# Moving the down-projection weights of a streamed mixture-of-experts block from SyncE's DMA queue to ScalarE's

## The chip, the cores and the metric

One core of a Trainium2 chip runs the whole kernel. The metric is the device time of one execution in microseconds (us). All data is float32: the weights are streamed from HBM (the chip's main memory) into the core's on-chip memory once, and the expert weights are more than three quarters of all bytes.

## The reference, cut to what matters

One decoder layer for 256 tokens of width 2048: an input projection, two groups of attention heads, an output projection, cross attention into 256 memory tokens, then a mixture of experts, and a final norm. The change touches the mixture of experts only:

```
# 32 experts, D_MODEL = 2048, D_EXPERT = 512; top-1 group of 8 experts, then top-2 in it
a = jnp.einsum('td,edf->tef', t, w_gate)            # w_gate (32, 2048, 512)
u = jnp.einsum('td,edf->tef', t, w_up)              # w_up   (32, 2048, 512)
act = jax.nn.silu(a) * u * combine[:, :, None]
y = jnp.einsum('tef,efd->td', act, w_down)          # w_down (32, 512, 2048)
...
return rms_norm(x + y, norm_final)
```

Every expert's three matrices are 4.19 MB each (2048 x 512 x 4 bytes), 12.58 MB per expert.

## The kernel before, in words

The kernel is written out by hand, one instruction stream for each engine, joined by semaphores. Each engine runs its own stream strictly in order. The streams of SyncE (SP), TensorE (PE), ScalarE (ACT), VectorE (DVE) and GpSimd (POOL) are the functions under `@block.sync`, `@block.tensor`, and so on.

**The experts' loop.** Experts 0 to 31 are processed one after the other, with 32 token slots each (all tokens fit in one pass over the experts with these inputs). On PE, `expert(n, ...)` does in this order: `combine` of the previous expert's first half of the tokens, `gate_up(0)` (the first half of the 2048 input rows against gate and up weights), `combine` of the second half, `gate_up(1)`, `gather` and `gather_turn` for the next expert's tokens, three transposes, `project_down`, which multiplies with the down weights in four quarters (j = 0 to 3). The last expert has its own function, `last_expert`, with four extra matmuls (`residual`) instead of the gather. ScalarE does the SiLU (sg), copies the gathered slots (x_slots), copies bank 6 (turned), and at the end copies the expert output from bank 7 to `y_sb`, which PE's next `combine` waits for. VectorE multiplies and adds the result to `x_res`.

**The buffers.** Gate and up weights have two buffers, `gu[0]` and `gu[1]`, of one whole expert each (8.39 MB). Down weights have one buffer for one expert (4.19 MB), in two halves `down0` and `down1`. The semaphores `gu_used0` and `gu_used1` count how often the first and second half of a gate/up buffer was read, `down_used0` and `down_used1` the same for the halves of the down buffer. `gu_loaded..` and `down_loaded0` to `down_loaded3` say that data have landed.

**The order of the loads.** Before the change all expert weights are issued by SP. `load_gate_up(e, side, used)` issues 4 DMAs of 2.1 MB: for each half b it waits for `gu_used{b}` to reach `used`, then issues gate and up. `load_down(e, used)` issues 4 DMAs of 1.05 MB, one for each quarter, and waits for `down_used0` and `down_used1`. In the steady loop (L411 to L415) SP issues expert e's gate and up once expert e-2 has read its own, and then expert e's down once expert e-1 has read its own; since SP runs in order, the gate and up of e+1 are issued only behind the down of e. On the queue the order is gate/up e, down e, gate/up e+1, down e+1. Nothing but the queue order decides what the DMA engines move next. The last load on that queue is the final gain `g_fin` (L428).

A row of gate or up of one DMA is 8 x 512 x 4 = 16384 bytes for each of 128 partitions, a row of down is 2048 x 4 = 8192 bytes.

Of the kernel before, what the change touches and what calls it, by code (L numbers as in the profile page):

```python
# [25 lines left out]
P = 128  # L26
# [7 lines left out]
EXPERTS = GROUPS * PER_GROUP  # L34
FE = 512
SLOTS = 32
NJ = P // SLOTS
MAX_PASSES = SEQ // SLOTS
AHEAD = 3
# [31 lines left out]
def chunk_cols(c):  # L71
    return KV_RANK + ROPE if c == KV_LAT else UN
# [40 lines left out]
def layer(nc, x, mem, positions, norm_mix, w_in, norm_q_lat, w_q_b, norm_kv_lat, w_kv_b,  # L113
# [6 lines left out]
    def S(name):  # L120
        if name not in sems:
            sems[name] = ctx.enter_context(nc.semaphore(name))
        return sems[name]

    with ctx:
# [4 lines left out]
        def place(name, shape, dt=F32, offset=None):  # L130
            size = 4
            for s in shape[1:]:
                size *= s
            if offset is None:
                offset = at[0]
                at[0] += size + (-size) % 64
            assert offset + size <= limit, (name, offset + size, limit)
            return nc.alloc_sbuf_tensor_at(name, shape, dt, offset=offset)
# [64 lines left out]
        down0 = place("down0", [P, 2, D], offset=e_at + 4 * 16 * 1024)  # L203
        down1 = place("down1", [P, 2, D], offset=a_lo_at)
# [106 lines left out]
        n = 0  # L311
# [30 lines left out]
        def _(sp):  # L342
# [13 lines left out]
            for u, (c, i) in enumerate(UNITS):  # L356
# [8 lines left out]
                dst = w_raw[:, u % RING, :, 0:chunk_cols(c)]  # L365
# [8 lines left out]
            def load_gate_up(e, side, used=None, halves=(0, 1)):  # L374

                wg = w_gate[0, e].rearrange("(p k) f -> p (k f)", k=KD)
                wu = w_up[0, e].rearrange("(p k) f -> p (k f)", k=KD)
                half = KD // 2 * FE
                for b in halves:
                    if used is not None:  # L380
                        sp.wait_ge(S(f"gu_used{b}"), used)
                    for m, w in enumerate((wg, wu)):
                        sp.dma_start(gu[side][:, b, m].rearrange("p k f -> p (k f)"),  # L383
                                     w[:, b * half:(b + 1) * half]).then_inc(
                                         S(f"gu_loaded{side}{b}"), 16)

            def load_down(e, used=None):
                wd = w_down[0, e].rearrange("(j p) d -> p j d", p=P)
                for b, dst in enumerate((down0, down1)):
                    if used is not None:  # L390
                        sp.wait_ge(S(f"down_used{b}"), used)
                    for jj in range(2):
                        sp.dma_start(dst[:, jj, :], wd[:, 2 * b + jj, :]).then_inc(  # L393
                            S(f"down_loaded{2 * b + jj}"), 16)

            sp.wait_ge(S("w_used"), START[MEM_O])
            sp.wait_ge(S("mem_scores"), MEM_HEADS)

            load_gate_up(0, 0)
            load_down(0)  # L400
            sp.wait_ge(S("w_used"), len(UNITS))
            sp.wait_ge(S("w_split"), len(UNITS))
            load_gate_up(1, 1)
            for e in range(2, AHEAD):
                load_gate_up(e, e % 2, e - 1)
                load_down(e - 1, e - 1)
            load_gate_up(AHEAD, AHEAD % 2, AHEAD - 1, halves=(0,))
            load_down(AHEAD - 1, AHEAD - 1)
            load_gate_up(AHEAD, AHEAD % 2, AHEAD - 1, halves=(1,))
            load_down(AHEAD, AHEAD)  # L410
            with sp.Fori(0, (EXPERTS - AHEAD - 1) // 2) as i:  # L411
                for m in range(2):
                    e = 2 * i + AHEAD + 1 + m
                    load_gate_up(e, (AHEAD + 1 + m) % 2, 2 * i + AHEAD + m)
                    load_down(e, 2 * i + AHEAD + 1 + m)  # L415
            sp.wait_ge(S("routed"), 1)
            total = sp.value_load(n_iter[0:1, 0:1], min_val=EXPERTS, max_val=MAX_PASSES * EXPERTS)
            with sp.If(total > EXPERTS):

                with sp.Fori(EXPERTS - 1, total - 1, EXPERTS) as before_:  # L420
                    with sp.Fori(0, EXPERTS // 2) as i:
                        for side in range(2):
                            load_gate_up(2 * i + side, side, before_ + 2 * i + side)
                            load_down(2 * i + side, before_ + 2 * i + 1 + side)
            total_1 = sp.value_load(n_iter[0:1, 1:2], min_val=EXPERTS - 1,
                                    max_val=MAX_PASSES * EXPERTS - 1)
            sp.wait_ge(S("gu_used1"), total_1)
# [477 lines left out]
        def _(sc):  # L905
# [268 lines left out]
            def slots_copy(n, first=False):  # L1174
                sc.wait_ge(S("gathered"), n + 1)
                if not first:
                    sc.wait_ge(S("slots_turned"), n)
                sc.activation(x_slots[:, :], ps[4][:, :], ACT.Copy).then_inc(S("slots_copied"), 1)  # L1178

            def expert(n, m=None):  # L1180

                sc.wait_ge(S("gu_used1"), n + 1)
                if m is not None:
                    sc.wait_ge(S("act_ready"), n)
                sc.activation(sg[:, :], ps[5][:, 0:P], ACT.Silu).then_inc(S("silu"), 1)  # L1185
                slots_copy(n + 1)
                sc.wait_ge(S("bank6_turned"), n + 1)
                if m is not None:
                    sc.wait_ge(S("combined"), TT * m + TT)
                    sc.wait_ge(S("down_used1"), n)  # L1190
                sc.activation(turned_6[:, :, :], ps[6][:, 0:(TT + 1) * P].rearrange(  # L1191
                    "p (t a) -> p t a", t=TT + 1), ACT.Copy).then_inc(S("bank6_copied"), 1)
                sc.wait_ge(S("down_used1"), n + 1)
                sc.activation(y_sb[:, :], ps[7][:, :], ACT.Copy).then_inc(S("y_copied"), 1)  # L1194

            slots_copy(0, first=True)
            sc.wait_ge(S("routed"), 1)
# [2 lines left out]
            before_last = sc.value_load(n_iter[0:1, 3:4], min_val=EXPERTS - 2,  # L1200
                                        max_val=MAX_PASSES * EXPERTS - 2)
            expert(0)
            with sc.Fori(0, before_last) as m:
                expert(m + 1, m)
# [550 lines left out]
        def _(gp):  # L1755
# [32 lines left out]
            def norms(cols, width, made, count):  # L1788

                gp.wait_ge(S(made), count)  # L1790
                for col in cols:
                    r = rstd[:, col:col + TT]
                    link(gp.tensor_scalar(r, sums[:, col:col + TT], 1.0 / width, EPS, ALU.mult, ALU.add))
                    ins = gp.tensor_tensor(r, r, minus_half[:, :], ALU.pow)
                ins.then_inc(S("rstd"), 1)
# [38 lines left out]
                    allow_small_or_imprecise_dtypes=True).then_inc(S("router_consts"), 1)  # L1834
            norms([SS_X2], D, "sums_made", 3)
            gp.wait_ge(S("rstd"), 7)
            def apply_gain(g):

                gp.wait_ge(S("last_added"), g + 1)
                cols = slice(g * UN, (g + 1) * UN)  # L1840
                gp.tensor_tensor(x_gain[:, g, :], x_res[:, 1, cols], g_fin[:, cols],
                                 ALU.mult).then_inc(S("gain_applied"), 1)

            gp.wait_ge(S("final_gain_loaded"), 16)
            for t in range(TT):
                apply_gain(t)
                gp.wait_ge(S("final_summed"), t + 1)
                link(gp.tensor_scalar(rstd[:, t:t + 1], sums[:, t:t + 1], 1.0 / D, EPS, ALU.mult,
                                      ALU.add))
                gp.tensor_tensor(rstd[:, t:t + 1], rstd[:, t:t + 1], minus_half[:, 0:1],  # L1850
                                 ALU.pow).then_inc(S("final_rstd"), 1)
            apply_gain(2)


# [24 lines left out]
```

## Time and profile before

| | |
|---|---|
| runs | 1423.21, 1419.56, 1421.71 us; median 1421.71 |
| the profiled execution | 1421.97 us, its span 1420.2 us |
| busy in the span | PE 75%, PE weight loads 45%, DVE 38%, ACT 24%, POOL 2% |
| moved | 481.69 MB in 87203 packets, 479.04 MB of it read from HBM |
| on SP's queue (q1) | 478.75 MB, 84.2% of the 16 DMA engines' time |
| on ACT's queue (q10) | 2.11 MB, 0.4% |
| experts' loop | from about 496 us to 1405 us |

The span is the time between the first and the last recorded instruction. The page's 40 slices are 35.5 us each. PE is the matrix engine and PEld its weight loads; an engine's name with q behind it (SPq, ACTq) is that engine issuing a DMA, L383 is line 383 of the kernel. In a row of waits, "A <- B" is time in which A's engine stood still until B was done.

### The profile page before, as it was taken

The numbers are of one execution on the slowest core, as the hardware profiler recorded it, in microseconds if no ns is written. First come the engines' busy times: TensorE is split into PE (matmuls) and PEld (weight loads), VectorE is DVE, ScalarE is ACT, GpSimd is POOL, SyncE is SP. The second block draws the span as 40 slices with busy tenths as digits, with TensorE's granted clock in tenths as the row PEclk, the third lists the DMA queues.
The fourth block names the chain that finished last, engine by engine and source line by source line (L and its number), as shares of the span: only waits on it lengthen the run. The fifth ranks groups of instructions, "written<-read, shape, count | busy, mean of one in ns | idle before, by whom it ended". The sixth has DMA issues, their size and how long they took to land.

```text
span 1420.2 us, 21509 instructions
## 1 busy us (share of the span) xinstructions
PE 1071.1 (75%) x8704; PEld 637.2 (45%) x8704; DVE 534.0 (38%) x1108; ACT 336.7 (24%) x608; POOL 33.1 (2%) x95
## 2 busy tenths in 40 slices
PE   7999999999998888665666666666566665666665
PEld 6888887888886633222222222222222222232222
DVE  5544576666654533222222222222222222222222
ACT  5554456665454400000000000000000000000002
POOL 1000001110001000000000000000000000000001
PEclk9999999999999888888888888888888888888888
DMA  7766653225558889999999999999999999999996
GB/s 234 256 201 184 178 164 119 95 70 193 188 181 317 334 358 424 427 427 427 426 424 429 425 427 425 425 426 427 427 425 425 427 427 426 426 425 428 426 426 265
DMA packets 87203, 481.69 MB, mean 339 GB/s; under 512 B 11318, under 2 KB 21692, under 8 KB 54012
## 3 DMA queue, kind: packets, MB, share of 16 engines
q1 hardware_dynamic: 86668, 478.75, 84.2%
q10 hardware_dynamic: 304, 2.11, 0.4%
q0 software_dynamic: 192, 0.31, 0.2%
q8 instruction: 25, 0.41, 0.1%
q14 instruction: 14, 0.11, 0.0%
HBM read 479.04 MB, written 2.10 MB: 339 GB/s over the span
## 4 chain that ended last, share of the span: by engine, by line
DMA 43%; PE 37%; SPq 6%; ACT 5%; DVE 3%; issue 2%; POOL 0%; ACTq 0%; POOLq 0%; DVEq 0%
DMA gu<-in_w_up 41%; PE ps L489 7%; PE ps L491 7%; PE ps L490 7%; PE ps L794 5%; SPq L383 5%; PE ps L847 4%; PE ps L775 2%; DMA down<-in_w_down 2%; DVE w_lo L1252 1%; SPq L393 1%; PE ps L784 1%; ACT x_slots L1178 1%; PE ps L456 1%; PE ps L512 1%
## 5 line engine op out<-in xcount | busy, mean ns | idle before, releaser
L794 PE MATMUL ps<-gu,xe 128*32 128x256 f32 x4096 | 319.9, 481 | 240.2 <-DMA gu<-in_w_up 239.2
L794 PEld LDWEIGHTS ps<-gu,xe 128*32 128x32 f32 x4096 | 153.7, 137 | 428.2 <-DMA gu<-in_w_up 286.4
L1646 DVE TENSOR_TENSOR x_res<-ps,x_res 128x512 f32<-128x512 f32 x248 | 154.0, 683 | 411.3 <-PE ps L804 411.3
L1252 DVE TENSOR_TENSOR w_lo<-w_raw,w_hi 128x1024 fp32r<-128x1024 f32 (+1 forms) x138 | 164.1, 1200 | 134.3 <-ACT w_hi L918 131.3
L489 PE MATMUL ps<-w_hi,a_hi 128*128 128x512 f32 (+1 forms) x512 | 202.0, 395 | 5.7 <-DVE w_lo L1252 3.8
L490 PE MATMUL ps<-w_lo,a_hi 128*128 128x512 f32 (+1 forms) x512 | 198.1, 387 | 0.0
L491 PE MATMUL ps<-w_hi,a_lo 128*128 128x512 f32 (+1 forms) x480 | 185.2, 386 | 0.0
L918 ACT ACTIVATE w_hi<-w_raw 128x1024 fp32r<-128x1024 f32 (+1 forms) x138 | 142.1, 1039 | 140.9 <-PE ps L491 132.4
L1185 ACT ACTIVATE sg<-ps 128x128 f32<-128x128 f32 x31 | 8.6, 278 | 613.2 <-PE ps L794 613.2
L847 PE MATMUL ps<-down,turned 128*32 128x512 f32 x1024 | 120.3, 609 | 26.7 <-ACT turned L1191 23.6
L489 PEld LDWEIGHTS ps<-w_hi,a_hi 128*128 128x128 f32 x512 | 97.0, 189 | 26.9 <-issue 5.5
L490 PEld LDWEIGHTS ps<-w_lo,a_hi 128*128 128x128 f32 x512 | 97.0, 189 | 18.0
L491 PEld LDWEIGHTS ps<-w_hi,a_lo 128*128 128x128 f32 x480 | 90.4, 188 | 18.2
L804 PE MATMUL ps<-y_sb,turned 32*128 32x512 f32 x496 | 71.7, 647 | 23.5 <-ACT y_sb L1194 23.5
L847 PEld LDWEIGHTS ps<-down,turned 128*32 128x32 f32 x1024 | 30.8, 110 | 94.4 <-issue 81.1
L1676 DVE TENSOR_TENSOR act<-sg,ps 128x128 f32<-128x128 f32 x31 | 8.9, 288 | 159.1 <-ACT sg L1185 159.1
L775 PE MATMUL ps<-h_nat,hot 128*32 128x512 f32 x512 | 62.5, 607 | 1.3 <-DVE hot L1628 1.3
L1637 DVE TENSOR_TENSOR xe<-ps,g_ffn 128x128 f32<-128x128 f32 x128 | 28.3, 283 | 78.1 <-PE ps L784 78.1
L804 PEld LDWEIGHTS ps<-y_sb,turned 32*128 32x128 f32 x496 | 20.0, 185 | 64.8 <-issue 38.8
L1194 ACT ACTIVATE y_sb<-ps 128x512 f32<-128x512 f32 x31 | 18.5, 597 | 124.8 <-PE ps L847 124.8
L784 PE MATMUL ps<-ident,x_slots 128*128 128x128 f32 x128 | 21.4, 291 | 23.0 <-ACT x_slots L1178 23.0
L784 PEld LDWEIGHTS ps<-ident,x_slots 128*128 128x128 f32 x128 | 13.7, 143 | 52.9 <-ACT x_slots L1178 52.9
(276 smaller groups left out, 771.4 us busy)
## 6 DMA issues: line engine op xcount, KB each, us to landing
gu<-in_w_gate SPq DMA_DIRECT2D x64, 2048.0 KB, 31.6
gu<-in_w_up SPq DMA_DIRECT2D x64, 2048.0 KB, 36.0
down<-in_w_down SPq DMA_DIRECT2D x128, 1024.0 KB, 23.6
w_raw<-in_w_in SPq DMA_DIRECT2D x56, 512.0 KB, 4.4
w_raw<-in_w_out SPq DMA_DIRECT2D x32, 512.0 KB, 3.8
w_raw<-in_w_mem_kv SPq DMA_DIRECT2D x16, 512.0 KB, 3.9
w_raw<-in_w_mem_q SPq DMA_DIRECT2D x8, 512.0 KB, 3.3
w_raw<-in_w_mem_o SPq DMA_DIRECT2D x8, 512.0 KB, 3.6
```

The lines of the kernel that those rows point to most:

```text
L383: sp.dma_start(gu[side][:, b, m].rearrange("p k f -> p (k f)"), w[:, b * half:(b + 1) * half]).then_inc(S(f"gu_loaded{side}{b}"), 16)
L489: pe.matmul(acc[t][:, 0:n], xh, wh, start=(k == 0), stop=False)
L490: pe.matmul(acc[t][:, 0:n], xh, wl, start=False, stop=False)
L491: mm = pe.matmul(acc[t][:, 0:n], xl, wh, start=False, stop=(k == kn - 1))
L775: mm = pe.matmul(ps[4][g * SLOTS:(g + 1) * SLOTS, :], hot[:, t, :], h_nat[:, t, 4 * g:4 * g + 4, :].rearrange("p k d -> p (k d)"), start=( ...
L784: mm = pe.transpose(ps[4][:, j * P:(j + 1) * P], x_slots[:, j * P:(j + 1) * P], ident[:, :])
L794: mm = pe.matmul(ps[5][j * SLOTS:(j + 1) * SLOTS, 0:2 * P].rearrange("s (m f) -> s m f", m=2), xe[:, k, :], gu[side][:, b, :, kk, j * P:(j ...
L804: return pe.matmul(ps[g][:, :], turned_6[rows, t, :], y_sb[rows, :], start=True, stop=True)
L847: mm = pe.matmul(ps[7][g * SLOTS:(g + 1) * SLOTS, :], act_t[:, j * SLOTS:(j + 1) * SLOTS], w[:, jj, g * UN:(g + 1) * UN], start=(j == 0), ...
L918: sc.activation(w_hi[:, u % RING, :, 0:n], w_raw[:, u % RING, :, 0:n], ACT.Copy).then_inc(S("w_rounded"), 1)
L1252: ve.tensor_tensor(w_lo[:, u % RING, :, 0:n], w_raw[:, u % RING, :, 0:n], w_hi[:, u % RING, :, 0:n], ALU.subtract).then_inc(S("w_split"), 1)
L1646: ins = ve.tensor_tensor(xs, ps[g][:, :], xs, ALU.add)
```

## The change

`load_down` goes from SP's stream. A new `load_first_down` issues expert 0's down weights on SP, where they were. All other experts' down weights are issued by ScalarE at the end of its `expert(n)`: behind the copy of `y_sb`, with a wait for `down_used0` in front (the wait for `down_used1` stands before the copy already). SP's loop has only `load_gate_up` left, with the same waits. The buffers, the semaphores and the computation stay as they were.

```diff
-            def load_down(e, used=None):
-                wd = w_down[0, e].rearrange("(j p) d -> p j d", p=P)
-                for b, dst in enumerate((down0, down1)):
-                    if used is not None:
-                        sp.wait_ge(S(f"down_used{b}"), used)
-                    for jj in range(2):
-                        sp.dma_start(dst[:, jj, :], wd[:, 2 * b + jj, :]).then_inc(
-                            S(f"down_loaded{2 * b + jj}"), 16)
+            def load_first_down():
+                wd = w_down[0, 0].rearrange("(j p) d -> p j d", p=P)
+                for j in range(NJ):
+                    sp.dma_start((down0, down1)[j // 2][:, j % 2, :], wd[:, j, :]).then_inc(
+                        S(f"down_loaded{j}"), 16)
...
             load_gate_up(0, 0)
-            load_down(0)
+            load_first_down()
             sp.wait_ge(S("w_used"), len(UNITS))
             sp.wait_ge(S("w_split"), len(UNITS))
             load_gate_up(1, 1)
             for e in range(2, AHEAD):
                 load_gate_up(e, e % 2, e - 1)
-                load_down(e - 1, e - 1)
-            load_gate_up(AHEAD, AHEAD % 2, AHEAD - 1, halves=(0,))
-            load_down(AHEAD - 1, AHEAD - 1)
-            load_gate_up(AHEAD, AHEAD % 2, AHEAD - 1, halves=(1,))
-            load_down(AHEAD, AHEAD)
+            load_gate_up(AHEAD, AHEAD % 2, AHEAD - 1)
             with sp.Fori(0, (EXPERTS - AHEAD - 1) // 2) as i:
                 for m in range(2):
                     e = 2 * i + AHEAD + 1 + m
                     load_gate_up(e, (AHEAD + 1 + m) % 2, 2 * i + AHEAD + m)
-                    load_down(e, 2 * i + AHEAD + 1 + m)
...
                 sc.wait_ge(S("down_used1"), n + 1)
                 sc.activation(y_sb[:, :], ps[7][:, :], ACT.Copy).then_inc(S("y_copied"), 1)
+                sc.wait_ge(S("down_used0"), n + 1)
+                wd = w_down[0, 1 if m is None else (m + 2) % EXPERTS].rearrange("(j p) d -> p j d", p=P)
+                for j in range(NJ):
+                    sc.dma_start((down0, down1)[j // 2][:, j % 2, :], wd[:, j, :]).then_inc(
+                        S(f"down_loaded{j}"), 16)
```

The order of the instructions in SP's steady loop before, one expert of the two that the loop holds (the line numbers are those of each kernel; an ISA row is a register or wait instruction; gu is the gate/up buffer, down the down buffer):

```order
L383 ISA [waits gu_used0]
L383 DMA gu_96<-in_w_gate 128x4096
L383 DMA gu_96<-in_w_up 128x4096
L383 ISA [waits gu_used1]
L383 DMA gu_96<-in_w_gate 128x4096
L383 DMA gu_96<-in_w_up 128x4096
L393 DMA down_98<-in_w_down 128x2048 [waits down_used0]
L393 ISA
L393 DMA down_98<-in_w_down 128x2048
L393 ISA [waits down_used1]
L393 DMA down_99<-in_w_down 128x2048
```

And the same loop now, two experts:

```order
L383 ISA [waits gu_used0]
L383 DMA gu_96<-in_w_gate 128x4096
L383 DMA gu_96<-in_w_up 128x4096
L383 ISA [waits gu_used1]
L383 DMA gu_96<-in_w_gate 128x4096
L383 DMA gu_96<-in_w_up 128x4096
L383 ISA [waits gu_used0]
L383 DMA gu_97<-in_w_gate 128x4096
L383 DMA gu_97<-in_w_up 128x4096
```

What moved: no down load and no wait for the down buffer stands between two experts' gate/up loads any more. ScalarE's loop over the experts, now:

```order
L1176 ACTIVATE sg<-ps 128x128 [waits act_ready]
L1166 REGISTER_ALU
L1169 ACTIVATE x_slots<-ps 128x512 [waits slots_turned,gathered]
L1180 ISA [waits bank6_turned]
L1182 ACTIVATE turned_130<-ps 128x384 [waits down_used1,combined]
L1185 ACTIVATE y_sb<-ps 128x512 [waits down_used1]
L1189 ISA [waits down_used0]
L1189 DMA down_98<-in_w_down 128x2048
L1189 ISA
L1189 DMA down_98<-in_w_down 128x2048
```

What moved: the four down loads (two shown) stand behind the copy of the expert output; before, the loop ended with that copy.

## Rows read from the trace of the kernel before

**Rows 1.** The page: DMA share and GB/s in 40 slices; DMA queues
```profile
DMA  7766653225558889999999999999999999999996
GB/s 234 256 201 184 178 164 119 95 70 193 188 181 317 334 358 424 427 427 427 426 424 429 425 427 425 425 426 427 427 425 425 427 427 426 426 425 428 426 426 265
```
**Rows 2.** The waits, 500 to 1400 us: us in total, times, longest
```profile
PEld ps L794 <- DMA gu<-in_w_up: 286.4, 57, 7.2
PE ps L794 <- DMA gu<-in_w_up: 239.2, 57, 6.4
...
PEld ps L847 <- DMA down<-in_w_down: 12.5, 18, 2.3
```
**Rows 3.** DMA queues in 1376 to 1391 us: packets, MB, share of 16 engines
```profile
q1 hardware_dynamic: 474, 6.38, 100.1%
```
**Rows 4.** Windows, one expert each: engines busy, PEclk, DMA share, GB/s
```profile
900.00:929.50 29.50, 19.66 (x219) 8.02 (x215) 8.56 (x24) 1.96 (x4) 0.00 (x0) 0.88 1.01 427
1332.00:1361.50 29.50, 20.13 (x199) 8.38 (x199) 7.12 (x20) 1.96 (x4) 0.00 (x0) 0.83 1.01 426
```
**Rows 5.** Windows at the loop's start: engines busy, PEclk, DMA share, GB/s
```profile
498.00:502.00 4.00, 4.00 (x52) 1.98 (x48) 0.52 (x2) 0.00 (x0) 0.00 (x0) 0.64 0.03 12
...
505.00:520.00 15.00, 12.97 (x155) 5.05 (x147) 5.56 (x17) 1.96 (x4) 0.00 (x0) 1.00 1.01 429
```
**Rows 6.** Timeline around the end of expert 30 and expert 31: start, us, engine
```profile
1362.13 3.66 PE L794 MATMUL ps<-gu,xe 128*32 128x256 f32 x64 [2.49 <-DMA gu<-in_w_up]
...
1370.01 3.64 PE L847 MATMUL ps<-down,turned 128*32 128x512 f32 x32 [0.79 <-ACT turned L1191]
...
1373.71 0.60 ACT L1194 ACTIVATE y_sb<-ps 128x512 f32<-128x512 f32 x1 [3.83 <-PE ps L847]
...
1374.36 1.14 PE L804 MATMUL ps<-y_sb,turned 32*128 32x512 f32 x8 [0.71 <-ACT y_sb L1194]
...
1391.67 5.35 PE L794 MATMUL ps<-gu,xe 128*32 128x256 f32 x64 [3.60 <-DMA gu<-in_w_up]
...
1400.91 3.64 PE L847 MATMUL ps<-down,turned 128*32 128x512 f32 x32
1404.62 0.60 ACT L1215 ACTIVATE y_sb<-ps 128x512 f32<-128x512 f32 x1 [5.55 <-PE ps L847]
```
**Rows 7.** SP's issues at the end of the experts' loop
```profile
1344.15 2.70 SPq L393 DMA_DIRECT2D down<-in_w_down  x4
1347.04 0.33 SPq L383 DMA_DIRECT2D gu<-in_w_gate  x1
1347.47 0.38 SPq L383 DMA_DIRECT2D gu<-in_w_up  x1
1348.04 3.63 SPq L383 DMA_DIRECT2D gu<-in_w_gate  x1
1351.76 4.19 SPq L383 DMA_DIRECT2D gu<-in_w_up  x1
1371.99 2.70 SPq L393 DMA_DIRECT2D down<-in_w_down  x4
```
**Rows 8.** ScalarE's only large DMA and its landing; SP's next issues
```profile
56.58 0.42 ACTq L1014 DMA_DIRECT2D mem_sb<-in_mem  x1
...
59.44 1.50 SPq L372 DMA_DIRECT2D w_raw<-in_w_in  x2
...
DMA to landing us min/median/max: 10.3/10.3/10.3
```
**Rows 9.** DMA queues in 57 to 59 us, 61 to 63 us and 63 to 65 us
```profile
q1 hardware_dynamic: 341, 0.67, 93.8%
...
q10 hardware_dynamic: 91, 0.75, 98.6%
...
q10 hardware_dynamic: 85, 0.70, 83.8%
q1 hardware_dynamic: 72, 0.15, 18.9%
```
**Rows 10.** Gate/up loads, all: us from issue to landing
```profile
DMA to landing us min/median/max: 7.2/35.5/40.0
```
**Rows 11.** Window 64 to 65 us, both queues at work
```profile
64.00:65.00 1.00, 1.00 (x7) 0.81 (x6) 1.00 (x1) 0.00 (x0) 0.00 (x0) 1.00 1.09 449
```

More of the change, by code:

```diff
@@ L423, in _ @@
                             load_gate_up(2 * i + side, side, before_ + 2 * i + side)
-                            load_down(2 * i + side, before_ + 2 * i + 1 + side)
             total_1 = sp.value_load(n_iter[0:1, 1:2], min_val=EXPERTS - 1,
```

## The prediction

> **What bounds the kernel now.** I began with the page's slices [rows 1]: from slice 17 (about 600 us) the DMA share reads 9 in every slice and the rate stands at 424 to 429 GB/s, while section 1 of the page gives no engine more than 75%. Then the waits [rows 2]: in the experts' loop PE and its weight loads stand still for gate/up data (the two rows count the same time twice, once for each), and for down data for 12.5 us in all. The windows of single experts confirm it: 29.5 us long, DMA share 1.01, 426 or 427 GB/s, PE busy for only some 20 us [rows 4]. One expert is 12.58 MB, and 12.58 MB / 0.427 MB per us = 29.5 us. So the loop is a queue of bytes that is never empty, and whoever asks for a time must ask three things: are the same bytes moved, is the queue ever empty, and how much work is left on PE when it has run out. The chain of waits cannot answer the last, the timeline at the end can [rows 6].
>
> **The end before.** Gate/up of expert 31 has landed at 1391.67, where PE starts on its second half [rows 6]. Behind it on the queue were only the down weights of 31, 4.19 MB, 9.8 us: the transfers end at about 1401.5. PE meanwhile needs 5.35 us of gate_up and some four us of small steps and residual matmuls, so that project_down starts at 1400.91 and takes its usual 3.64 us [rows 6]; the down load is hidden. y_sb is copied at 1405.22, and everything behind it (combine, norm, store) is the same before and after.
>
> **The change, part by part.**
> SP loses 124 down issues of 0.68 us (2.70 us for four [rows 7]) and its waits for the down buffer. SP stands waiting most of the time, so this is worth nothing by itself. What follows from it: gate/up of e+2 is no longer held until project_down of e has half finished; it is issued right behind gate_up of e, some 7 us sooner. No buffer is added, so gate/up can be ahead by two experts at most, as before, but it now stands in its queue before the down weights of e+1.
> ScalarE gains 4 issues for each of 31 experts. Its one large DMA took 0.42 us to issue [rows 8]; SP's pitch gives 0.68. That is 1.7 to 2.7 us per expert, behind the y_sb copy, so PE's combine isn't held up, and before ScalarE's next work (the SiLU behind both gate_up halves, 1.14 + 3.66 + 1.14 + 3.66 = 9.6 us later at the soonest). Even issues that stall as SP's did (up to 4.19 us [rows 7]) would come to under 17 us, and would be felt only in part. I take 0. The added wait for down_used0 is met when that for down_used1 is.
> The down weights of e+1 are now asked for when all of project_down(e) and the copy are done, not when its first half is: 1.8 + 0.7 us later. What counts is how the two queues share the engines.
>
> **How the queues share.** Only once does the trace show ScalarE's queue at work beside SP's: the 2.1 MB load of 56.58 us, landed after 10.3 us [rows 8]. In 61 to 63 us it has the engines alone; in 63 to 65 us both move, 85 packets of 8 KB (0.70 MB) beside 72 of 2 KB (0.15 MB) [rows 9]. That is packet for packet, not byte for byte. The packets of gate/up are 16 KB rows (in 1376 to 1391 us, 474 packets, of which 50 are tiny completions, carry 6.38 MB, 15 KB each [rows 3]), those of down 8 KB rows. Packet for packet, gate/up gets two thirds and down one third. The Trainium skill says the same of the switching ("DMA: Bandwidth & Descriptors", Queues, rings and completion order: each DMA engine takes turns between its rings at packet granularity); by bytes in equal parts the sum would be 9.8 us, the first rival below, instead of 14.7.
>
> At one third, 0.142 MB/us, the down weights need 29.5 us from the first byte. Between one expert's down landing and the next one's first byte lie the last quarter of project_down (0.91), the copy and its hand-over (0.71), and the start of a DMA (7.2 us is the shortest landing of 2.1 MB [rows 10], less 4.9 us for the bytes: 2.3, part of it at the landing end): 3.5 to 4 us. 29.5 + 3.8 is more than the 29.5 us of an expert's bytes, so down becomes what PE waits for, by some 11 us per expert, and gate/up runs ahead until its two buffers are full and its queue runs dry; then down has the engines alone and catches up. As long as gate/up has 1.6 MB (3.8 us) in its queue when a down load lands, no time is lost: 29.5 us per expert as before. At the start of the loop the transfers pause before 502 us, waiting for the first expert, and are busy from 505 us on [rows 5]; that stays. **Steady part: 0.**
>
> **The end after, which makes the sum.** Gate/up has run ahead, so what is left at the end is down alone, and down cannot run ahead: one buffer. When down of 29 lands, in the extreme case only down of 30 and 31 are unmoved, 19.6 us of transfers; all else has been moved without a pause, so this is at 1401.5 - 19.6 = 1381.9. From there PE goes: last quarter 0.91, copy and hand-over 0.71, then twice a whole expert at PE's own pace. One is 1.14 + 3.66 + 1.14 + 3.66 (combines and gate_up) + 4.22 (1365.79 to 1370.01) + 3.64 + 0.71 = 18.2 us, all from [rows 6]. Down of 30 and 31 take 9.8 + 2.3 us and their issues and just hide in it. 1381.9 + 1.6 + 36.4 = 1419.9 against 1405.2: **+14.7 us**. The near bound: gate/up of 31 and down of 30 land together at 1401.5 - 9.8 = 1391.7; 1.6 + 18.2 behind that is 1411.5, **+6.3**. The far one: both experts' gate_up at 5.35 instead of 3.66 us, as after PE's idle time in [rows 6]: 4 x 1.7 more, +21.5. I take +14.7, because a gate/up queue with two thirds of the rate runs dry first. On the profiled execution of 1421.97 that is 1436.7, on the median of 1421.71 it is **1436.4 us**.
>
> **Rivals.**
> 1. *Gate/up lands last.* If down gets half of the bytes or more (for it: in 61 to 63 us ScalarE's queue had 98.6% [rows 9] although SP had issued more from 59.44 on [rows 8]), down is in early and gate/up of 31 ends the transfers at 1401.5 instead of 1391.67. PE's 13.5 us behind it stay: +9.8, 1431.5. Or it ends at the near bound, +6.3, 1428. Chance 0.30.
> 2. *Starved down.* If gate/up gets more than two thirds, or the start of a DMA is longer than 2.3 us behind full engines (issued at 56.58 [rows 8], ScalarE's load had moved nothing before 59 [rows 9]), the gate/up queue is empty when down lands, and both stand still for 3.8 us. At one expert in three: 10 x 3.8 = 38, 1421.7 + 14.7 + 38 = 1474; at every expert 1550. It decides as soon as less than 1.6 MB is queued at the landing. Chance 0.10.
> 3. *More rate from two queues, faster.* One microsecond with both at work shows 449 GB/s [rows 11] against 427. Behind 502 us the loop has 30 x 8.39 + 31 x 4.19 = 382 MB, 894 us at 427; at 449 it is 44 us less, and with the tail 1421.7 - 44 + 14.7 = 1392. It decides from 1.6% on. Against it: the engines are at 1.01 busy with one queue already, and 63 to 65 us around that microsecond show 0.85 MB in 2 us. Chance 0.04.
> 4. *Nothing.* Same bytes, same engines: if gate/up doesn't run ahead, and the last down still comes last, the end is as before, 1421.7. The Trainium skill speaks for this (same page, Issuing engines are not separate DMA queues: DMAs of several engines interleave on the same 16, and a second one saves only issue time). The new queue order speaks against it: SP no longer holds gate/up of 31 until project_down(29). Chance 0.06.
>
> **How the numbers follow.** Forecast 0.50, rivals 0.30, 0.10, 0.04, 0.06. A measurement of this kernel can tell 0.3%, 4.3 us. The forecast and rivals 1 and 2 are slower by more: 0.90; rival 4 the same 0.06; rival 3 faster 0.04. The range takes in the near bound, 1428, and the far one, 1443, with two or three gaps of 3.8 us: 1427 to 1452; rivals 2, 3 and 4, 0.20, lie outside.
>
> **What would show it.** In the changed kernel's profile: ScalarE's queue at about 130 MB and SP's at about 349; the windows of single experts still 29.5 us and 427 GB/s; PE's wait for down grown from 12.5 us to some 300, that for gate/up nearly gone; single down loads landing 20 to 30 us after the issue; in the last 40 us a DMA share well under 1, with PE at 18 us for each of the two last experts. Gate/up waits as before and a last gate/up landing near 1401 would make it rival 1; windows under 427 GB/s in mid-loop, rival 2; over 430, rival 3.

## The result and the profile after

The changed kernel takes 1435.87 us (median of 5, 1430.77 to 1437.76) against 1421.84 us of the kernel before in the same series: 14.0 us more, ratio 1.0091 with a 95% interval of 1.0073 to 1.011. In a second series (e5 below) it was 1432.26 against 1423.4 us, ratio 1.007 (1.0048 to 1.0091). So the medians put the cost of the change at 14 us once and at 9 us once. The prediction was 1436.4 us.

The profiled execution took 1436.69 us, its span is 1435.0 us. The page, against [rows 1]: the DMA share, the rates, and the queues.

```profile
DMA  7766653225558799999999999999999999999994
GB/s 228 249 209 182 182 165 120 92 80 185 190 178 339 298 386 423 427 425 418 430 425 427 424 422 426 427 427 408 425 426 427 427 426 424 426 429 424 426 397 176
...
q1 hardware_dynamic: 68812, 348.72, 61.8%
q10 hardware_dynamic: 18160, 132.14, 22.3%
```

348.72 MB are left on SyncE's queue, 132.14 MB are on ScalarE's, and from slice 15 to slice 37 (counted from 0) the engines are almost as busy as before (two slices fall short, 418 and 408 GB/s). The last two slices are not: 397 and 176 GB/s, where [rows 1] has 426 and 265. The same in windows (columns as in [rows 4]): 740 us of the loop's middle of the kernel before, then of the changed one,

```profile
600.00:1340.00 740.00, 471.20 (x4975) 194.37 (x4975) 193.42 (x500) 49.13 (x101) 0.00 (x0) 0.85 1.01 426
```

```profile
600.00:1340.00 740.00, 479.13 (x4975) 177.66 (x4975) 193.50 (x500) 49.09 (x100) 0.00 (x0) 0.79 1.01 425
...
1390.00:1400.00 10.00, 5.66 (x24) 0.61 (x24) 0.00 (x0) 0.00 (x0) 0.00 (x0) 0.53 0.68 282
1400.00:1410.00 10.00, 9.28 (x120) 4.04 (x120) 4.21 (x7) 0.60 (x1) 0.00 (x0) 0.79 0.85 342
1410.00:1420.00 10.00, 9.33 (x79) 3.46 (x71) 1.05 (x3) 1.36 (x3) 0.00 (x0) 1.00 0.19 79
```

In the middle 425 against 426 GB/s: almost nothing lost. The bytes moved in 520 to 1380 us say how much, first before, then changed:

```profile
DMA packets 33800, 366.44 MB, mean 426 GB/s; under 512 B 3754, under 2 KB 3754, under 8 KB 3754
```

```profile
DMA packets 33464, 365.42 MB, mean 425 GB/s; under 512 B 3712, under 2 KB 3712, under 8 KB 3712
```

1.02 MB fewer is 2.4 us of the engines' time (0.64 MB and 1.5 us in e5, the changed kernel's second trace). At the end the engines run at 0.68, 0.85 and 0.19 while PE is busy; that is the larger part. The waits in the loop, against [rows 2]:

```profile
PEld ps L838 <- DMA down<-in_w_down: 314.5, 59, 7.2
PE ps L838 <- DMA down<-in_w_down: 244.0, 57, 6.3
```

No row for gate/up is left; PE waits for down instead, and for about as long in all (244.0 us against 239.2 in [rows 2]). Who is waited for has changed altogether, and the mean time of an expert has hardly changed. How the queues share (bytes and packets in 904 to 910, 912 to 918 and 918 to 926 us):

```profile
q1 hardware_dynamic: 164, 2.42, 94.9%
q10 hardware_dynamic: 15, 0.12, 4.8%
...
q10 hardware_dynamic: 334, 2.44, 97.7%
q1 hardware_dynamic: 12, 0.15, 5.8%
...
q1 hardware_dynamic: 160, 2.36, 69.3%
q10 hardware_dynamic: 146, 1.03, 31.0%
```

First gate/up nearly alone, while down pauses; then down nearly alone, because gate/up has filled its buffers; then both, 160 packets beside 146, which is 2.36 MB beside 1.03 MB. (The packet counts hold a few tiny completions.) The timeline at the end, against [rows 6]:

```profile
1371.23 1.06 PE L838 MATMUL ps<-down,turned 128*32 128x512 f32 x8 [0.61 <-DMA down<-in_w_down]
1372.36 0.60 ACT L1185 ACTIVATE y_sb<-ps 128x512 f32<-128x512 f32 x1 [4.65 <-PE ps L838]
1372.54 1.92 ACTq L1189 DMA_DIRECT2D down<-in_w_down  x4
...
1398.21 1.93 PE L838 MATMUL ps<-down,turned 128*32 128x512 f32 x8 [0.52 <-DMA down<-in_w_down]
1400.21 0.60 ACT L1185 ACTIVATE y_sb<-ps 128x512 f32<-128x512 f32 x1 [13.62 <-PE ps L838]
1400.38 2.04 ACTq L1189 DMA_DIRECT2D down<-in_w_down  x4
...
1402.88 4.26 PE L785 MATMUL ps<-gu,xe 128*32 128x256 f32 x64
...
1408.14 3.66 PE L785 MATMUL ps<-gu,xe 128*32 128x256 f32 x64
...
1415.69 3.64 PE L838 MATMUL ps<-down,turned 128*32 128x512 f32 x32
1419.40 0.60 ACT L1211 ACTIVATE y_sb<-ps 128x512 f32<-128x512 f32 x1 [5.55 <-PE ps L838]
```

Both gate_up halves of expert 31 start with no wait for data; down 31 is asked for only at 1400.38, and PE then needs a whole expert at its own pace. The last y_sb is copied at 1420.0 us, before at 1405.22: 14.8 us later. Of these, 2.1 us were there before the change could cost anything: expert 0's y_sb is copied at 515.85 us, where the trace of before has 513.77, and what PE does up to there is the same code on data loaded as before. That this is chance is seen over the runs: the same copy stands between 509.7 us (e3) and 516.4 us (e7) in the traces of all kernels here. So the traces are compared below from this copy on. From expert 0's copy to expert 31's it is 904.2 us against 891.5, **12.7 us more**. They split like this: up to expert 30's copy 885.0 against 860.5 us (24.4 more), and then 19.2 against 30.9 us for the last expert (11.7 given back).

### The profile page after: what moved, and what is told of

It reads as the page before. It is cut to its first block, busy times and chain, and to the rows that moved or that the text cites. A ratio compares the mean times of both kernels' runs of the same rounds, so it can differ in the third digit from the quotient of the medians.

```text
span 1435.0 us, 21555 instructions
## 1 busy us (share of the span) xinstructions
PE 1083.3 (75%) x8704; PEld 619.8 (43%) x8704; DVE 534.1 (37%) x1108; ACT 336.9 (23%) x608; POOL 33.1 (2%) x95
## 3 DMA queue, kind: packets, MB, share of 16 engines
q1 hardware_dynamic: 68812, 348.72, 61.8%
q10 hardware_dynamic: 18160, 132.14, 22.3%
## 4 chain that ended last, share of the span: by engine, by line
DMA 49%; PE 35%; ACT 4%; DVE 3%; ACTq 2%; issue 2%; POOL 0%; POOLq 0%; DVEq 0%
DMA down<-in_w_down 49%; PE ps L480 7%; PE ps L482 7%; PE ps L481 7%; PE ps L838 5%; PE ps L785 4%; ACTq L1189 2%; DVE w_lo L1248 1%; PE ps L795 1%; PE ps L766 1%; PE ps L447 1%; PE ps L503 1%; ACT w_hi L909 1%; ACT head_junk L1047 1%; ACT y_sb L1185 0%
## 5 line engine op out<-in xcount | busy, mean ns | idle before, releaser
L838 PE MATMUL ps<-down,turned 128*32 128x512 f32 x1024 | 166.8, 759 | 268.4 <-DMA down<-in_w_down 244.0
L785 PE MATMUL ps<-gu,xe 128*32 128x256 f32 x4096 | 265.1, 417 | 1.0 <-DVE xe L1633 1.0
L785 PEld LDWEIGHTS ps<-gu,xe 128*32 128x32 f32 x4096 | 134.3, 120 | 167.4 <-issue 98.8
L838 PEld LDWEIGHTS ps<-down,turned 128*32 128x32 f32 x1024 | 26.5, 119 | 368.8 <-DMA down<-in_w_down 314.5
L795 PE MATMUL ps<-y_sb,turned 32*128 32x512 f32 x496 | 94.1, 836 | 23.6 <-ACT y_sb L1185 23.6
L795 PEld LDWEIGHTS ps<-y_sb,turned 32*128 32x128 f32 x496 | 24.7, 231 | 83.0 <-issue 49.6
L1169 ACT ACTIVATE x_slots<-ps 128x512 f32<-128x512 f32 x32 | 19.1, 597 | 44.7 <-PE ps L766 44.7
## 6 DMA issues: line engine op xcount, KB each, us to landing
gu<-in_w_up SPq DMA_DIRECT2D x64, 2048.0 KB, 24.5
down<-in_w_down ACTq DMA_DIRECT2D x124, 1024.0 KB, 14.8
```

Of the source, the lines that this page charges most:

```text
L785: mm = pe.matmul(ps[5][j * SLOTS:(j + 1) * SLOTS, 0:2 * P].rearrange("s (m f) -> s m f", m=2), xe[:, k, :], gu[side][:, b, :, kk, j * P:(j ...
L795: return pe.matmul(ps[g][:, :], turned_6[rows, t, :], y_sb[rows, :], start=True, stop=True)
L838: mm = pe.matmul(ps[7][g * SLOTS:(g + 1) * SLOTS, :], act_t[:, j * SLOTS:(j + 1) * SLOTS], w[:, jj, g * UN:(g + 1) * UN], start=(j == 0), ...
```

## The experiments

**e1: one queue, gate/up ahead.** The kernel before, with each down load issued behind the gate/up load of the expert after it.

```diff
-                    load_down(e, 2 * i + AHEAD + 1 + m)
+                    load_down(e - 1, 2 * i + AHEAD + m)
...
+            load_down(EXPERTS - 1, EXPERTS - 1)
```

> All down loads are on SyncE's queue again, but behind the gate/up loads of the expert after, so that gate/up runs ahead and nothing is shared between two queues. Theory A (the time went to the end of the loop, because gate/up has run ahead and the last down load needs its buffer): the order gate/up 31, down 30, down 31 costs the near bound of the prediction, +6 us (4 to 9), and single experts still take 29.5 us at 427 GB/s. Theory B (the second queue itself costs, by sharing or by ScalarE's issues): as the kernel before, within 2 us.

Measured: 1430.89 us against 1421.9, ratio 1.0052 (1.0037 to 1.0068), which is 5 to 10 us. Its waits and its middle:

```profile
PE ps L844 <- DMA down<-in_w_down: 232.4, 120, 7.5
```

```profile
600.00:1340.00 740.00, 505.28 (x4999) 172.14 (x4991) 193.47 (x500) 49.05 (x100) 0.00 (x0) 0.78 1.01 426
```

There is no second queue here, and half and more of the loss is there, with 232 us of waits for down (244 in the changed kernel) and the same rate in the middle. Gate/up ahead of down is enough to lose at the end. Theory B falls as the whole cause; whether the second queue adds a few us of its own the times can't tell, since this interval overlaps that of the changed kernel's second series. The 9 us are over the near bound of 6.3, and the trace shows why. From expert 0's copy to expert 31's it is 900.1 us, 8.7 more than before. PE had been waiting for expert 30's down weights, and at the start of expert 31 its granted clock is 0.68 (1393.9 to 1400.6 us):

```profile
1393.88 2.09 PE L801 MATMUL ps<-y_sb,turned 32*128 32x512 f32 x8 [0.70 <-ACT y_sb L1191]
1395.90 4.79 PE L791 MATMUL ps<-gu,xe 128*32 128x256 f32 x64
```

At the full clock the two take 1.14 and 3.66 us [rows 6]. These 2.1 us on top of 6.3 make 8.4.

**e2: down rows of 4 KB.** The changed kernel, each down DMA cut in two by columns, on both queues; PE waits for 32 instead of 16 per quarter.

```diff
+                    for c in range(2):
+                        cs = slice(c * D // 2, (c + 1) * D // 2)
+                        sc.dma_start((down0, down1)[j // 2][:, j % 2, cs], wd[:, j, cs]).then_inc(
+                            S(f"down_loaded{j}"), 16)
```

> The changed kernel with each down load cut in two, with rows of 4 KB in place of 8 KB; the bytes are the same. If the two queues take turns packet by packet, down gets one fifth of the rate beside gate/up (4 KB to 16 KB) in place of one third, gate/up is out when down lands, and the engines stand still: 30 to 130 us slower than the changed kernel, with windows of single experts clearly under 427 GB/s. If they share by bytes, or by time in equal parts, the time is that of the changed kernel within 3 us.

Measured: 1514.12 us, ratio to the kernel before 1.0673 (1.0633 to 1.0713), some 80 us above the changed kernel. The queues in 1040 to 1044 us, and the middle window:

```profile
q1 hardware_dynamic: 100, 1.38, 81.1%
q10 hardware_dynamic: 103, 0.36, 22.1%
```

```profile
600.00:1340.00 740.00, 445.64 (x4589) 167.08 (x4593) 179.74 (x469) 45.61 (x93) 0.00 (x0) 0.77 0.95 391
```

100 packets beside 103, 1.38 MB beside 0.36: packet for packet again, and now down has a fifth. The rate falls to 391 GB/s: this is the starved down of the prediction's rival 2, made to happen by cutting the rows. The cut also doubles the number of down DMAs. The packet counts speak for the rows as the cause, and the doubled gate/up DMAs of e3 cost nothing like it, but no run has twice the DMAs with rows of the old size.

**e3: gate/up rows of 8 KB.** The changed kernel, each gate/up DMA cut in two, PE waiting for 64 instead of 32.

> The changed kernel with each gate/up load cut in two, with rows of 8 KB in place of 16 KB. Packet by packet, down then gets one half of the rate: it lands within 20 us, PE's waits move from down (244 us) back to gate/up, windows stay at 427 GB/s, and the end is rival 1 of the prediction, gate/up of 31 landing last: +8 to +18 us against the kernel before. By bytes or time: waits for down stay at some 240 us.

Measured: 1441.02 us (of five runs one at 1433.24, the profiled one, and four from 1440.57 to 1441.22), ratio 1.0135 (1.0118 to 1.0152): +19 us. Queues in 1040 to 1044 us, waits, and the middle:

```profile
q1 hardware_dynamic: 118, 0.85, 51.2%
q10 hardware_dynamic: 117, 0.83, 49.7%
```

```profile
PE ps L788 <- DMA gu<-in_w_up: 237.0, 29, 13.9
...
PE ps L841 <- DMA down<-in_w_down: 31.4, 12, 4.1
```

```profile
600.00:1340.00 740.00, 450.47 (x4947) 184.42 (x4939) 194.27 (x502) 49.03 (x100) 0.00 (x0) 0.83 1.01 422
```

With rows of equal size the bytes are shared equally, and the 240 us of waits went back from down to gate/up. That was rival 1, and it shows that this rival was decided by the row sizes. The time is higher than its 9.8 us. The trace is of the fastest execution, 11 us over the kernel before, and its expert 0 was copied 4 us earlier than before, at 509.72 us; from there to expert 31's copy it is 906.8 us, 15.4 more. The second half of gate/up 31 lands at 1402.85 us:

```profile
1402.85 5.50 PE L788 MATMUL ps<-gu,xe 128*32 128x256 f32 x64 [6.88 <-DMA gu<-in_w_up]
```

That is 893.1 us after the first copy, where before has 877.9 (1391.67 - 513.77): 15.2 us later, nearly the whole of the loss. Two things make it. The rate in the middle is 422 in place of 426 GB/s at the same DMA share of 1.01, and 1% of the loop's 890 us is about 9 us. The other 6 are the order, less than rival 1's 9.8, since gate/up 31 is still not the very last: in 1403 to 1408 us ScalarE's queue moves 1.45 MB more. That the smaller rows cost the rate is what the two rates suggest; it wasn't measured by itself.

**e4: the last eight experts in the old order.** The changed kernel, but the down loads of experts 24 to 31 are issued by SyncE, each between the gate/up loads as before; ScalarE issues 1 to 23. (The code for more than one pass, which these inputs don't take, isn't served in e4 and e9.)

```diff
+            for e in range(24, EXPERTS):
+                load_gate_up(e, e % 2, e - 1)
+                load_down(e, e)
```

> The changed kernel up to expert 23; from expert 24 on, down loads are issued by SyncE in the order of the kernel before. Theory A (the steady part is free, the loss is at the end): most of the 14 us comes back, 0 to +6 us against the kernel before. Theory C (the loss is spread over the loop, by sharing, half a microsecond per expert): 24/32 of it stays, +10 or more.

Measured: 1427.73 us, ratio 1.0037 (1.0019 to 1.0055): 3 to 8 us above the kernel before. Two windows at the hand-over, where down 24 waits for its buffer and gate/up 25 waits behind it:

```profile
1184.00:1194.00 10.00, 7.69 (x79) 2.87 (x75) 2.77 (x12) 1.96 (x4) 0.00 (x0) 1.00 0.36 136
1187.00:1189.00 2.00, 0.98 (x7) 0.75 (x7) 0.86 (x5) 0.79 (x2) 0.00 (x0) 1.00 0.00 0
```

The DMA engines stand at 0.36 in these 10 us, 6.4 us of engine time lost in one pause. From expert 0's copy to expert 31's the trace has 898.8 us, 7.3 more than before, so the pause is most of this kernel's loss, and the end is the old one (30.3 us for the last expert, 30.9 before). The experts on two queues cost little: in 520 to 1180 us 280.29 MB are moved, before 281.22, which is 2.2 us. The times alone would not exclude Theory C (24/32 of the 9 us of the second series is 7 us); the trace does, as it shows a single pause where C has a cost in every expert.

**e9: only the last two.** The same with experts 30 and 31.

> The changed kernel with only the last two down loads, 30 and 31, issued by SyncE in the order of the kernel before: down 30 behind gate/up 30 and in front of gate/up 31. Theory A: gate/up 31 waits for down 30 to be asked for, which costs one pause of about 4 to 6 us (as at the hand-over of e4, 5.75 us), and the end is then the kernel before's; together +4 to +7 us, 5 or more less than the changed kernel. Theory C (the loss is spread over the loop): as the changed kernel, +10 to +14.

Measured: 1429.83 us against 1421.84, ratio 1.0048 (1.003 to 1.0067): 8.0 us more (4 to 10), above Theory A's 4 to 7 and below Theory C's 10 to 14. It was run in a series of its own, so it stands beside e4 only by its ratio. Its ten times spread from 1422.26 to 1432.54 us, and the trace is of one of the two fastest, 1422.35. That trace has no pause and no loss:

```profile
1380.00:1390.00 10.00, 9.19 (x112) 3.58 (x112) 3.36 (x8) 0.60 (x1) 0.00 (x0) 1.00 1.01 430
1390.00:1400.00 10.00, 8.15 (x77) 3.81 (x74) 2.77 (x5) 0.77 (x2) 0.00 (x0) 0.83 0.99 413
```

From copy to copy it is 891.7 us, as before (891.5), with 29 experts on two queues and only the last two in the old order. The fastest executions of the changed kernel took 1430.77 and 1429.96 us in the two series. So this is the strongest evidence that the loss sits at the end. What the slower executions of e9 lost, and whether it was the pause, is not shown.

**e5: the changed kernel again.** No edit.

> The changed kernel once more, unedited, as the measure for the next two, which differ from it by a few microseconds: 1431 to 1438 us.

Measured: 1432.26 us against 1423.4. Its trace comes nearer to the extreme case of the prediction than the first one: expert 0's y_sb is copied at 513.83 us, expert 30's at 1399.80, expert 31's at 1417.44, and the last two experts take 21.1 and 17.6 us, both at PE's own pace with no wait for data. The 3.5 us between them are mostly the clock. PE had stood waiting for down (5.44 us before the last quarter of expert 29), the granted clock is 0.50 in 1370 to 1385 us, and expert 30 begins with

```profile
1378.87 2.09 PE L795 MATMUL ps<-y_sb,turned 32*128 32x512 f32 x8 [0.81 <-ACT y_sb L1185]
1380.89 5.74 PE L785 MATMUL ps<-gu,xe 128*32 128x256 f32 x64
```

where expert 31, at 1.00, takes 1.14 and 3.66 us for the same. Windows:

```profile
1390.00:1400.00 10.00, 7.78 (x83) 2.91 (x79) 2.33 (x10) 1.96 (x4) 0.00 (x0) 1.00 0.44 164
1395.00:1400.00 5.00, 3.79 (x36) 1.12 (x40) 1.28 (x6) 0.97 (x2) 0.00 (x0) 1.00 0.05 18
```

903.6 us from the first copy to the last, 12.2 more than before, with nothing of it from ahead of the loop (513.83 against 513.77 us).

**e6: the final gain later.**

```diff
             sp.wait_ge(S("gu_used1"), total_1)
+            sp.wait_ge(S("down_used1"), total_1)
```

> In the changed kernel the 1 MB load of the final gain sits on SyncE's queue behind the last gate/up load, and takes turns with down 30 from 1389.5 to 1394 us; here SyncE waits for down_used1 of expert 30 before it issues it. Theory A (everything that delays down 30 delays the end): 2.4 us less than the changed kernel (1.05 MB / 0.427). If the end is set by PE or by gate/up: no difference.

Measured: 1429.76 us, 2.5 less than e5, but the ratios to the kernel before, 1.006 (1.0037 to 1.0082) and 1.007 (1.0048 to 1.0091), overlap. Inconclusive by the times, though the size is the expected one. The trace points the same way: expert 30 is copied 882.3 us after expert 0, where the two traces of the changed kernel have 885.0 and 886.0. That the gain load shares the engines with down 30 in the changed kernel is on record for 1389.5 to 1394 us:

```profile
q10 hardware_dynamic: 136, 0.97, 52.2%
q1 hardware_dynamic: 123, 0.92, 49.6%
```

**e7: the first half of down sooner.**

```diff
+                sc.wait_ge(S("down_used0"), n + 1)
                 for j in range(NJ):
+                    if j == 2:
+                        sc.wait_ge(S("down_used1"), n + 1)
+                        sc.activation(y_sb[:, :], ps[7][:, :], ACT.Copy).then_inc(S("y_copied"), 1)
```

> In the changed kernel ScalarE issues the first two of the four down loads before it copies y_sb, as soon as the first half of the down buffer is read, some 2 us sooner; its issues (0.9 us) lie beside project_down. Theory A (steady part bound by bytes, end bound by down 30 and the chain behind it): 0 to 2 us less than the changed kernel, all of it at the end. If the late request cost something for every expert (2 us x 30): up to 14 us less, back to the kernel before.

Measured: 1433.32 us, 1.1 above e5, ratio 1.0071 (1.0046 to 1.0095). Asking sooner in each of 31 experts brings nothing that the times can tell. The single trace does show a small gain: 366.47 MB in 520 to 1380 us, as many as before, and 900.9 us from copy to copy against 903.6 and 904.2, while its expert 0 was copied late, at 516.38 us. So 2 or 3 us may hang on the time of the request, not the 14 of the second theory; one trace doesn't show it.

**e8: the old waits kept.** The changed kernel, with SyncE still waiting for the down buffer before each gate/up load, as the kernel before did by its order.

```diff
+                    sp.wait_ge(S("down_used1"), 2 * i + AHEAD + m)
                     load_gate_up(e, (AHEAD + 1 + m) % 2, 2 * i + AHEAD + m)
```

> One part of the change alone: down loads on ScalarE's queue, but SyncE still waits for the down buffer before it issues the next gate/up, as the kernel before did, so gate/up can't run ahead. Theory A (two queues take turns by packet, and gate/up ahead is what fills the engines while down pauses): down and gate/up of the same expert land together, nothing is queued behind, and each expert has the engines idle: 60 to 120 us slower than the kernel before, down and gate/up waits both large, windows under 400 GB/s. Theory D (it was the lookahead alone that cost, the queues don't matter): as the kernel before, within 3 us.

Measured: 1572.24 us, ratio 1.1061 (1.1031 to 1.1091), +149 us. Windows in mid-loop:

```profile
900.00:910.00 10.00, 1.93 (x8) 0.20 (x8) 0.00 (x0) 0.00 (x0) 0.00 (x0) 0.57 1.02 431
910.00:920.00 10.00, 7.65 (x64) 2.62 (x68) 2.48 (x4) 0.60 (x1) 0.00 (x0) 0.57 0.56 208
920.00:930.00 10.00, 8.49 (x119) 4.00 (x115) 3.86 (x11) 1.36 (x3) 0.00 (x0) 1.00 1.00 428
```

While down is being waited for, all that was queued runs out (1.02), then comes the pause (0.56). The loss is over the 60 to 120 us that I had put down, and gate/up was hardly waited for; I had not worked out the pause per expert (149 / 30 = 5 us, rather than 2 to 4). Theory D falls: with down on a queue of its own, gate/up must be free to run ahead, or each expert pays the pause.

No version beat the kernel before; e9's fastest executions equal it. e6 put on top of e4 or e9 wasn't tried; there the gain load stands behind the last down load anyway.

## Why the prediction was right

- **What bounds the kernel.** Right. In the middle 426 GB/s before and 425 after at a DMA share of 1.01, although PE's waits changed their object. e8 and e2, the two that lost much, are the ones whose middle window is under 400 GB/s (365 and 391).
- **How the queues share.** Right, and the step on which all rested: packet for packet. It had been read from one ScalarE load with 8 KB beside 2 KB [rows 9]. e2 (100 beside 103 packets at 16 and 4 KB) and e3 (118 beside 117 at equal size) show it. The Trainium skill's rule ("DMA: Bandwidth & Descriptors", Queues, rings and completion order) agrees with the traces as far as the switching goes; here a packet of the trace was one row.
- **Steady part: 0.** Nearly right: 2.4 and 1.5 us by the bytes of the two traces (and under 1 us in e9's, 366.11 MB), against 12 to 13 us in all. The average expert in the changed kernel took 885.0 / 30 = 29.5 us. But the windows of single experts are not all 29.5 us, as the prediction said: the copies of y_sb mostly stand some 36 and 20 to 28 us apart in turn (after expert 1: 21.9, 36.7, 24.5, 35.8, 20.6, 36.1), since an expert whose down load met little gate/up is followed by one that met much. And single down loads took 14.8 us in the median (4.7 to 33.6), not 20 to 30. Neither touches the sum by itself, but it makes the end a matter of where in this alternation expert 29 falls: it took 20.7 us in the first trace and 33.8 in e5's.
- **Issues on ScalarE: 0.** Right: 1.92 us for the four of expert 30, and the issues in e2, twice as many, end well inside ScalarE's idle time. SyncE's own issues got shorter (0.66 us at most, for a gate/up load, where 4.19 had been), which is worth nothing, as said.
- **The end, +14.7.** Right in mechanism: gate/up had run ahead, and down 31 was asked for so late that PE still had a whole expert to do. The size is partly luck. In the loop the two traces give +12.7 and +12.2, and the first of them has 2.1 us more from ahead of the loop, which made the total of 14 come out so close; the second series has 9. And two terms were off in opposite directions. In e5 expert 29 is copied at 1378.73 us, 4.8 sooner than the sum's 1383.5 (1381.9 + 1.6): not everything but down 30 and 31 had been moved by then. The two experts behind it took 21.1 + 17.6 = 38.7 us, 2.3 more than the sum's 36.4, because PE began expert 30 at the low clock, which the sum had only in its far bound. In the first trace the two errors are larger: expert 29 is copied at 1372.96 us, gate/up 31 and the gain load were still moving beside down 30, and expert 30 took 27.9 us with waits for down in it. The gain load on SyncE's queue was a term that I had not seen: behind down 31 it was free, beside down 30 it isn't.
- **The rivals.** "Gate/up lands last" did not happen, and e3 shows what would have made it. "Starved down" did not happen but was near: rows of 4 KB (e2) bring it, and one wait more (e8) brings like pauses. "More rate from two queues" did not happen: 425 GB/s. "Nothing" did not happen. The Trainium skill's rule behind it, that issuing from several engines only saves issue time ("DMA: Bandwidth & Descriptors", Issuing engines are not separate DMA queues), agrees with the traces in the rate, 425 against 426 GB/s. The 9 to 14 us came from the order in which the loads land, which is no matter of the rate.

## What to carry to other kernels

In a loop bound by bytes, look at the end, not at the waits. Here moving a load to another queue changed which wait was long and left the rate of the loop almost alone, but it changed what was left to do on PE when the bytes ran out: 12 us in the last two experts. The good end had one down load behind the last gate/up load, hidden beside PE's work on that gate/up. The bad ends (the changed kernel and e1) had two down loads there and one buffer for them, so the second could only be asked for when the first was used up. And where two queues share the engines, count packets, not bytes: the two queues moved like numbers of rows, and the one with the small rows and the single buffer starved in e2.

## What the runs showed of the hardware

- Two queues of different issuers took turns one packet (here one row of a partition) each: 160 beside 146 at 16 and 8 KB, 100 beside 103 at 16 and 4 KB, 118 beside 117 at 8 and 8 KB (each count with a few tiny completions). In that window of e2 the rate rises and falls about every 0.77 us, and one 16 KB row and one 4 KB row on each of 16 engines take 0.76 us at 430 GB/s: one row each, not several, before the turn. Cutting the rows of one load in half (and so doubling its DMAs) moved the kernel by 80 us.
- The total rate was the same with one queue and with two, 425 to 426 GB/s with rows of 16 and 8 KB, and 422 with 8 KB alone, at a DMA share of 1.01 each time.
- TensorE's granted clock was 0.50 (1.2 GHz) in 1370 to 1385 us of e5, where PE had waited 5.34 and 5.44 us for down before its last two quarters, and the same half of a gate_up took 5.74 us there and 3.66 us in the next expert at 1.00 (2.4 GHz). In mid-loop PE waits for data in any case; at the end of e5 it was 3 of the 12 us, in combine and gate_up of expert 30.
